# Four query and key tiles of a two-layer transformer step move into neighbourhood attention's first twelve steps

## Time and profile before

| | |
|---|---|
| median of 3 runs | 2887.59 us (2887.43 to 2888.29) |
| the profiled execution | its span 2885.2 us, 2.4 us below the median of the runs |
| PE, PEld busy | 2841.8 us (98%), 2658.3 us (92%) |
| DVE, ACT, POOL busy | 2112.8 us (73%), 1190.9 us (41%), 347.7 us (12%) |
| input projection from its fourth tile | 508.9 to 593.9 us |
| V projection | 593.9 to 622.4 us |
| neighbourhood attention, 20 steps | 622.4 to 672.5 us |
| its output projection | 672.5 to 700.8 us |

### The profile page before, as it was taken

The page is one execution under the profiler, slowest core; times in us unless marked ns, Lnnn a source line. Parts: engine busy times, 40 slices in busy tenths (PEclk is TensorE's granted clock), DMA queues, the critical chain, the costliest instruction groups (busy, mean ns, idle before and its releaser), DMA issues. The chain is left out here.

```text
span 2885.2 us, 46747 instructions
## 1 busy us (share of the span) xinstructions
PE 2841.8 (98%) x18154; PEld 2658.3 (92%) x18154; DVE 2112.8 (73%) x4053; ACT 1190.9 (41%) x2212; POOL 347.7 (12%) x436
## 2 busy tenths in 40 slices
PE   8999999999999999999999999999999999999998
PEld 5999999978789999999999998798887988999998
DVE  5898987766768989778878775755747467866856
ACT  5433535254666334356334354223233144533433
POOL 1000003120031000021000022202112033000001
PEclk9999999999999999999999999999999999999999
DMA  7544343521014433424433222324223231422221
GB/s 258 147 150 132 107 127 119 180 74 47 23 46 131 152 119 105 130 79 116 130 100 103 92 96 94 111 94 125 68 87 116 81 132 37 105 78 88 76 86 66
DMA packets 94238, 303.52 MB, mean 105 GB/s; under 512 B 10753, under 2 KB 21281, under 8 KB 93121
## 3 DMA queue, kind: packets, MB, share of 16 engines
q1 hardware_dynamic: 67328, 223.03, 23.8%
q0 software_dynamic: 21296, 63.58, 8.0%
q10 hardware_dynamic: 5392, 13.92, 1.3%
HBM read 285.14 MB, written 7.49 MB: 101 GB/s over the span
## 5 line engine op out<-in xcount | busy, mean ns | idle before, releaser
L2566 PE MATMUL ps<-g,w 128*128 128x320 f32 x4224 | 624.8, 308 | 0.0
L2566 PEld LDWEIGHTS ps<-g,w 128*128 128x128 f32 x4224 | 620.6, 187 | 0.8
L2533 PE MATMUL ps<-h,w 128*128 128x320 f32 x3744 | 578.3, 309 | 8.4 <-ACT swu L1022 4.6
L2533 PEld LDWEIGHTS ps<-h,w 128*128 128x128 f32 x3744 | 556.0, 188 | 10.3 <-ACT swu L1022 5.7
L2533 PE MATMUL ps<-e,w 128*128 128x320 f32 x2808 | 437.3, 309 | 0.1
L2533 PEld LDWEIGHTS ps<-e,w 128*128 128x128 f32 x2808 | 418.2, 188 | 0.4 <-DMA e<-tsum 0.4
L1541 DVE TENSOR_TENSOR w<-raw,w 128x1024 fp32r<-128x1024 f32 (+1 forms) x243 | 277.5, 1146 | 160.9 <-ACT w L915 144.7
L2714 PE MATMUL ps<-w,h 128*128 128x512 f32 x1596 | 367.4, 391 | 0.1
L2714 PEld LDWEIGHTS ps<-w,h 128*128 128x128 f32 x1596 | 298.1, 188 | 62.7 <-ACT rg L1486 1.0
L928 ACT ACTIVATE w<-w2s 128x512 fp32r<-128x512 f32 x312 | 194.1, 631 | 275.2 <-DVE w2s L1693 84.2
L915 ACT ACTIVATE w<-raw 128x1024 fp32r<-128x1024 f32 x123 | 128.9, 1061 | 264.2 <-PE ps L2400 130.9
(11 more groups left out here) (305 smaller groups left out, 3672.4 us busy)
## 6 DMA issues: line engine op xcount, KB each, us to landing
raw<-in_ws SPq DMA_DIRECT2D x303, 512.0 KB, 3.7
cond<-in_ada POOLq DMA_DIRECT2D x80, 512.0 KB, 3.9
raw<-in_ws SPq DMA_DIRECT2D x96, 384.0 KB, 3.1
raw<-in_ada SPq DMA_DIRECT2D x32, 512.0 KB, 3.6
cond_em<-in_ada POOLq DMA_DIRECT2D x16, 512.0 KB, 3.9
e<-tsum POOLq DMA_DIRECT2D x12, 640.0 KB, 6.3
ada<-in_ada SPq DMA_DIRECT2D x5, 1024.0 KB, 17.9
rst<-in_state ACTq DMA_DIRECT2D x4, 1024.0 KB, 4.8
```

The source lines that it names most:

```text
L2533: mm = pe.matmul(ps[:, 4 * s + bank, 0:HT], w2[:, at // 2, wi, c:c + P], rhs(k, ri), start=start and k + wi + ri == 0, stop=(k == 3 and wi ...
L2566: mm = pe.matmul(pair_half(pr, half), w2[:, slot_of(n), wi, c:c + P], half_of(g2[:, k, ri, :], half), start=k + wi + ri == 0, stop=(k == n ...
```

## The change

- The block order becomes: five latent tiles, query tiles 0 and 1, key tiles 0 and 1, the rotary tile, V, then query and key tiles 2 and 3 (heads 4 to 7). The projection has 10 tiles in place of 14; squares, sums and broadcasts move up by as many.
- The last four tiles are projected in token halves of 320, eight halves of eight groups of three matmuls, all in bank 7. The 64 groups are dealt over the first twelve steps: eight ahead of step 0's transposes, then two or three ahead of the transposes and two or three behind them. A half starts when the one before it is evacuated; ACT evacuates halves 0, 1, 4, 5, DVE halves 2, 3, 6, 7.
- The four blocks are split by ACT and DVE around the first units and at units 8 and 14, the output projection's first two among them. DVE's copies of V tile 4 go behind unit 2 in place of unit 3.
- The context output goes to 128 free columns of bank 5, and ACT copies it twice (`octx`), so that DVE reads its rest from there. V tile 4 goes to bank 6.
- The latents are split behind neighbourhood attention: ACT's high parts ahead of its splits for the output projection, DVE's low parts between its additions.
- Three condition blocks and two memsets move behind the rotary key on DVE, the last condition load behind the power on POOL. Two bias buffers and the conditions' row lie in 12 KB that a smaller descriptor area for POOL's transfers leaves free.

```diff
-EM_PAIR = [0, 1, 3, 2, 0] + [(e - 4) % 3 for e in range(5, 14)]
-V_BANK = [2, 3, 4, 5, 7]
+EM_PAIR = [0, 1, 3, 2, 0, 1, 2, 0, 1, 0]
+EM_SQUARES = {3: (0,), 4: (1,), 5: (2,), 6: (3,), 7: (4,)}
+EM_SUMS = {4: (0, 1), 5: (2,), 6: (3,), 7: (4,)}
+V_BANK = [2, 3, 4, 5, 6]
+DENSE_SLOTS = [(8, 0)] + [((3, 2), (3, 3), (2, 3))[i % 3] for i in range(10)] + [(3, 0)]
+DENSE_ACT = (0, 1, 4, 5)
+DENSE_SPLITS = {8: 18, 14: 19}
+LATENTS = (3, 4, 0, 1, 2)
...
 ACT, behind the first units
             exp_unit(1, True)
+            split(n0 + EM_V + 6)
...
+            dense_outs(0)
             pt_evac(0, True)
             pt_evac(1, True)
+            split(n0 + EM_V + 7)
             for g in range(2, NU):
                 exp_unit(g, True)
+                if g % 2 == 0 and g >= 4:
+                    dense_outs(g - 2)
                 if g >= 4:
                     pt_evac(g - 2, True)
...
+            for j in LATENTS:
+                latent_hi(j)
             for m in range(4):
                 split(n0 + 18 + m + LEAD, (n0 + 18 + m + LEAD) % RING)
...
 DVE
                 normalise(g)
-                if g == 3:
-                    dve.wait_ge(wt_free, done(n0 + 17))
+                if g == 2:
+                    dve.wait_ge(wt_free, done(n0 + EM_V + 3))
                     v_rows(5, slice(0, P), 4)
                     v_rows(3, high, 4, low).then_inc(v_odd, 1)
+                    split(n0 + EM_V + 6)
+                if g == 3:
+                    split(n0 + EM_V + 7)
...
+                dense_outs(g - 2)
+                if g - 1 in DENSE_SPLITS:
+                    split(n0 + DENSE_SPLITS[g - 1])
...
             for j in range(4):
                 split(n0 + 18 + j + LEAD)
+                if j:
+                    for c in ((), LATENTS[0:2], LATENTS[2:4], LATENTS[4:])[j]:
+                        latent_lo(c)
                 dve.wait_ge(wt_free, done(n0 + 18 + j))
...
 PE
+            def dense_step(i):
+                d, k = divmod(i, KD)
+                j, h = divmod(d, 2)
+                n = n0 + EM_DENSE + j
+                if k == 0:
+                    if h == 0:
+                        have(n)
+                    if d:
+                        pe.wait_ge(em_ev, EM_TILES - 1 + d)
+                for wi, ri in ((0, 0), (0, 1), (1, 0)):
+                    mm = pe.matmul(ps[:, 7, 0:HT], w2[:, slot_of(n), wi, k * P:(k + 1) * P],
+                                   half_of(h2[:, k, ri, :], h), start=(k == 0 and wi == 0 and ri == 0),
+                                   stop=(k == KD - 1 and wi == 1))
+                if k == KD - 1:
+                    mm.then_inc(wt_free if h else dense_mm, 1)
...
                 for g in range(0, NU, 2):
                     if g + 4 < NU:
                         pair_scores(g + 4)
+                    dense(g // 2, 0)
...
                     weight_mm(g, True)
                     weight_mm(g + 1, True)
+                    dense(g // 2, 1)
+                    if g % 10 not in (0, 2):
                         pair_values(g - 2, True)
...
+            pe.wait_ge(c_lo, 5)
             tok_tiles(n0 + 22, 1, lambda k, ri: ckv2[:, k, ri, :], 2, range(6), lambda t: 2 + t,
-    nc = bacc.Bacc("TRN2", target_bir_lowering=False, num_devices=1)
+    nc = bacc.Bacc("TRN2", target_bir_lowering=False, num_devices=1, dynamic_dma_scratch_size=4096)
```

More of the change, by code:

```diff
@@ L69 @@
 FFN_AT.append(NBLOCKS)
-EM_PAIR = [0, 1, 3, 2, 0] + [(e - 4) % 3 for e in range(5, 14)]
-V_BANK = [2, 3, 4, 5, 7]
+EM_PAIR = [0, 1, 3, 2, 0, 1, 2, 0, 1, 0]
+EM_TILES = len(EM_PAIR)
+EM_V = EM_TILES
+EM_DENSE = EM_V + 4
+EM_SQUARES = {3: (0,), 4: (1,), 5: (2,), 6: (3,), 7: (4,)}
+EM_SUMS = {4: (0, 1), 5: (2,), 6: (3,), 7: (4,)}
+V_BANK = [2, 3, 4, 5, 6]
+DENSE_SLOTS = [(8, 0)] + [((3, 2), (3, 3), (2, 3))[i % 3] for i in range(10)] + [(3, 0)]
+DENSE_END = [sum(map(sum, DENSE_SLOTS[:i])) + sum(DENSE_SLOTS[i][:v + 1]) for i in range(len(DENSE_SLOTS))
+             for v in range(2)]
+DENSE_HALVES = 8
+LATENTS = (3, 4, 0, 1, 2)
+DENSE_ACT = (0, 1, 4, 5)
+DENSE_SPLITS = {8: 18, 14: 19}
+DENSE_AT = {next(i for i, end in enumerate(DENSE_END) if end >= KD * (d + 1)): d for d in range(DENSE_HALVES)}
 NA_WINDOW = {1: (0, 192), 2: (64, 256), 3: (192, 256), 4: (320, 192)}
@@ L812, in _ @@
             norm_pow(1)
-            for b in range(2, ADA_EM):
+            for b in range(2, ADA_EM - 1):
                 condition_load(ADA_FFN[0] + b)
@@ L1190, in _ @@
             act.dma_start(ckvr[:, :, 0:PAST], a["cache_ckv"]).then_inc(em_ld2, 16)
-            for e in range(13):
+            for e in range(EM_TILES - 1):
                 if e > 1:
[L1193 to L1203, removed]
+                    split(n0 + e + LEAD)
+                for j in EM_SQUARES.get(e, ()):
                     act.wait_ge(em_ev, j + 1)
@@ L1208, in _ @@
                     act.activation(esq[:, j % 2, :], src, ACT.Square).then_inc(esq_done, 1)
-            act.wait_ge(em_ev, 13)
-            for e in range(4):
+                act.wait_ge(wt_free, done(n0 + e))
+                src = pair(EM_PAIR[e])
+                if 5 <= e < 7:
+                    act.activation(qa[e - 5], src, ACT.Copy, scale=NAD ** -0.5).then_inc(em_ev, 1)
+                else:
+                    dst = cqr[:, e, :] if e < 3 else ckvr[:, e - 3, PAST:] if e < 5 else ka[:, e - 7, PAST:]
+                    act.activation(dst, src, ACT.Copy).then_inc(em_ev, 1)
+            act.wait_ge(em_ev, EM_TILES - 1)
+            for e in range(2):
                 act.dma_start(a["new_k"][:, e], ctx_of(ka[:, e, PAST:])).then_inc(out_done, 16)
-            for j in range(3):
-                split(n0 + 13 + j + LEAD, (n0 + 13 + j + LEAD) % RING)
-            act.wait_ge(wt_free, done(n0 + 13))
+            for n in range(EM_TILES + 1, EM_TILES + 4):
+                split(n0 + n)
+            act.wait_ge(wt_free, done(n0 + EM_TILES - 1))
             act.dma_start(va_na[4], a["cache_v"]).then_inc(em_ld, 16)
@@ L1232, in latent_hi @@
                     act.activation(ckv2[:, j - 3, 0, :], ckvr[:, j - 3, :], ACT.Copy).then_inc(c_hi, 1)
[L1234 to L1243, removed]
+            split(n0 + EM_V + 4)
+            split(n0 + EM_V + 5)
             def exp_unit(g, na):
@@ L1324, in _ @@
             act.wait_ge(pv_mm, NU)
-            o_ctx(3)
+            na_ctx(3)
+            act.wait_ge(em_ev, EM_TILES - 1 + DENSE_HALVES)
+            for e in range(2, 4):
+                act.dma_start(a["new_k"][:, e], ctx_of(ka[:, e, PAST:])).then_inc(out_done, 16)
+            for j in LATENTS:
+                latent_hi(j)
             for m in range(4):
@@ L2072, in _ @@
             rstd_diag(NT, 1, e_var, e_pow, e_diag, NT)
-            split(n0 + 13 + LEAD)
-            dve.wait_ge(wt_free, done(n0 + 13))
+            split(n0 + EM_TILES + 1)
+            dve.wait_ge(wt_free, done(n0 + EM_TILES - 1))
             dve.wait_ge(e_rb, 2)
@@ L2683, in _ @@
             halves((n0, n0 + 1, n0 + 2), EM_PAIR[0:3], 1)
-            for e in range(3, 14):
+            for e in range(3, EM_TILES):
                 if e >= 4:
@@ L2810, in pair_values, with dense @@
                             mm.then_inc(pv_mm, 1)
+            def dense_step(i):
+                d, k = divmod(i, KD)
+                j, h = divmod(d, 2)
+                n = n0 + EM_DENSE + j
[10 more added lines that the diff above has]
+                    mm.then_inc(wt_free if h else dense_mm, 1)
+            def dense(i, v):
+                if i < len(DENSE_SLOTS):
+                    at = 2 * i + v
+                    for step in range(DENSE_END[at - 1] if at else 0, min(DENSE_END[at], KD * DENSE_HALVES)):
+                        dense_step(step)
             def attend_pairs():
@@ L3187, in stream_blocks @@
         put(tiles(wi[:, o + e * P:o + (e + 1) * P]))
-    for e in range(8):
+    for e in (0, 1, 4, 5):
         put(tiles(wi[:, e * P:(e + 1) * P]))
@@ L3192, in stream_blocks @@
     token_major(wi[:, 2 * na:3 * na])
+    for e in (2, 6, 3, 7):
+        put(tiles(wi[:, e * P:(e + 1) * P]))
     wo = w["mix_w_out"][0]
```

122 lines of the change are left out of this document (79 added, 43 removed).

## The result

The changed kernel takes 2892.30 us (median of 20 runs, 2889.63 to 2896.63) against 2887.55 for the kernel before on the same chips: 4.75 us more, ratio 1.0017 with a 95% interval of 1.0012 to 1.0023. The forecast was 2889.6, range 2882.9 to 2894.5, and "same within 0.2%" its likeliest case. The time is inside the range, at its upper part, and inside the 0.2%; the interval says that the kernel is slower and not equal.

What follows compares the result with a forecast made beforehand. TensorE, busy 98% of the span, bounds the kernel, so only its waits matter. Moved matmuls cancel (-28.0 + 28.0) and small terms sum to +2.0 us on 2885.2; with 2.4 us to the runs' median, 2889.6 us, range 2882.9 to 2894.5.

Steps and rivals of the forecast that it cites:

- Edits taken at nothing, (a): Norm's chain moved four tiles forward: diagonal ready at 556.2, PE at broadcast at 556.7, so hidden; 0 (0 to 1.5 us).
- Steps 0 and 1: First two attention steps: PE waits 0.9 us for unit 2, 3.2 for unit 3; wait grows 2.0 to 4.1, +2.1.
- The clock: Attention, after the new 3.2 us PE wait: loss from a fall to half clock, a third taken, +0.4 us (0 to 2).
- Waits for an evacuation: Step 5: half 4 waits until VectorE has evacuated half 3 from bank 7; +1.1 us (0 to 1.5).
- Gaps and changes of kind: PE's gaps in steps 2 to 11 go, -3.7 us; dense groups in 22 places add 0.1 each, +2.2 us.
- The last eight steps: End of neighbourhood attention: both engines start ahead, so part of 1.03 us of PE waits goes; -0.4 us (0 to -1).
- Behind attention: Output projection to latent projection: last latent low part ends about when PE asks for it; +0.3 us (0 to 2).
- (f), the descriptor area: POOL's software transfers: smaller area keeps every other address, at most three transfers are open at once; 0.
- (1): Rival: dense work fills everything, no wait in steps 0 and 1, changes of kind free; -4.7 us, 2882.9; chance 0.15.
- (2): Rival: dense groups empty the array in 22 places at 0.32 us, 7.0 instead of 2.2; 2894.4; chance 0.08.
- (3): Rival: each half waits for its evacuation as half 3 does, seven times 1.1 us; 2896.2; chance 0.04.
- (4): Rival: the change does not hide its work, every gap stays and groups only add; +6.1 us, 2893.7; chance 0.05.

Runs made afterwards that it cites:

- experiment 2: Changed kernel with VectorE's two copies of V tile 4 behind unit 3 and its split parts behind units 4 and 5: 2888.56 us, ratio to before 1.0006.
- experiment 3: Changed kernel with half 3 evacuated by ScalarE and ScalarE's split of block 19 at unit 13 instead of 14: 2891.91 us, ratio to before 1.0013.
- experiment 11: The changed kernel as it is, run once more: 2892.29 us, ratio to before 1.0015.
- experiment 1: Changed kernel with the latents' variance one condition block earlier and POOL's last two condition loads behind the power: 2891.29 us, ratio to before 1.0012.
- experiment 6: Kernel of experiment 4 with ten more places for dense groups, one group behind each step's first unit's transposes: one run, 2882.37 us.
- experiment 8: Kernel of experiment 4 with dense groups shifted in steps 0 and 11, more of them behind the transposes: 2884.88 us, ratio to before 0.9990.
- experiment 5: Kernel before the change with only the smaller descriptor area (4096) for POOL's transfers: 2887.24 us, ratio 1.0001.
- experiment 9: Kernel of experiment 8 with the first latent's ten sums behind tile 3, apart from the second's: 2882.59 us, ratio to before 0.9982.
- experiment 4: Changed kernel with the edits of experiments 1, 2 and 3, plus ScalarE's split of block 17 behind unit 4's exponential: 2884.78 us, ratio to before 0.9989.
- experiment 7: Kernel of experiment 4 with 184 of the 192 moved dense matmuls left out, evacuations and waits kept: attention takes 58.19 us.

## Why the forecast came out 2.7 us low, term by term

The case was the forecast's: the moved matmuls cancel and small terms decide. The sum was +2.0; in the profile it is +5.45 for these stretches, in the medians +4.75. Of what it said would show it, the wait in step 1 (3.04 us) and the one behind half 3 (0.97) came. A projection without a wait did not, and attention takes 81.75 us (595.58 to 677.33), where 79.1 to 80.1 were named. Its own signs of being wrong came true twice: the ten steps run at 4.85 us each (4.7 was the bound), and the clock stays low for some 3.4 us (3). That the range held is luck in part: in the profile four terms came out 4.3 us above the forecast together, and three others 0.9 below it.

- **Edits taken at nothing, (a): 0 became 1.86.** This is the largest miss, a term that was put at nothing; its bound of 1.5 was passed in the profile. I had counted "hidden by half a microsecond" from the one execution of before, in which VectorE waited at most 0.53 for a load. The four profiles with this chain (the first, experiments 2, 3 and 11) show that the landing of the loads varies and that the wait is 0 to 1.72 us; half a microsecond is no margin over a chain of 13 loads, each waiting for the block two before.
- **Steps 0 and 1: +2.1 became +2.0** (3.70 us of waits against 1.70). The forecast had 0.9 us for unit 2 and 3.2 for unit 3; it is 0.66 and 3.04, for the reason given: this was the forecast's best mechanism, and experiment 2 confirms it.
- **The clock: +0.4 became +1.5.** It fell behind the 3.04 us. I weighed the dense groups close ahead of the wait as holding it; they did not. In the other profiles with that wait (experiments 1, 3 and 11) it fell as well. The Trainium skill's page "TensorE: Matmul & The Clock Gate", section "Part 1: The HAM clock gate", has the slow clock as the default that activity lifts, which the forecast read as a sure fall. The traces agree at 3.04 us of wait (four of four), and at waits of 0.65 and 0.49 (experiment 2) they show 1.00 throughout.
- **Waits for an evacuation: +1.1 became +1.73.** Half 3's was 0.97. Half 5's (0.76) I had missed: I had counted what PE does between two halves, and not that ScalarE's split of block 19 stands ahead of half 4's evacuation (experiment 3).
- **Gaps and changes of kind: -3.7 + 2.2 became -2.0.** This is what is left of the twelve steps when the other terms are taken off. The net was near, both terms too large. A change of kind costs 0.03 where it was measured (experiment 6) and not 0.1: a gap counted from start to start holds the end of the transposes, which nothing can fill but which a dense group behind them does not pay again. The idle time of the busy view, 2.32 us for these steps, was the nearer count. The same Trainium skill page, section "Step-by-step: what each phase is for", gives 0 for a change of kind by its rule that weights load ahead; the trace has 0.03, nearer to that than the row that I took.
- **The last eight steps: -0.4 became +0.34.** No engine starts ahead: VectorE's scores wait for the transposes four units back, which stand behind the dense groups. Experiment 8 shows it: two groups shifted take 0.84 us off.
- **Behind attention: +0.3 became 0.** The last low part ended at 704.3, PE asked at 705.59.
- **(f), the descriptor area**, costs nothing in the kernel before (experiment 5). Of the rivals, (1) is what the kernel of experiment 9 reaches (2882.59, forecast 2882.9) once the orders are mended, though by other terms: -1.5 in steps 0 and 1, -1.9 in steps 2 to 11, -0.5 in the last eight, against -2.0, -3.7 + 1.1 and -0.4; (2) is out by experiments 4 and 6; (3) happened for two halves; (4) is out, since experiment 4 has no waits where before had 2.32 us.

## What to carry to other kernels

Work moved into an engine's gaps was worth about those gaps as its idle time shows them, a few microseconds here, and each queue that it brings work to can take them back: list, for each engine, what stands ahead of the instruction that the bound engine waits for next. A chain that had time to spare before the move has to be given its margin again; one trace shows one landing of its loads and not the spread. A single wait of 3.04 us on TensorE was paid here one and a half times or more, once as a wait and once in the clock.

## What the runs showed of the hardware

- After the 3.04 us wait the granted clock fell from 1.00 to 0.50 (2.4 to 1.2 GHz) in four profiles of four, in three during the wait, in one 0.9 us behind it. It stayed there for 3.4 to 6.8 us, most of it under full PE work. From the transposes behind the wait to the values PE took 4.65 to 5.83 us, against 3.26 at a clock of 1.00 (experiment 2): 1.4 to 2.6 us lost.
- In experiment 7, where PE was busy for 6.84 of 10.62 us, the clock also fell behind a wait of 1.84 us, and again behind one of 2.08.
- A run of matmuls of one column can take the clock down although PE shows no wait: 1.5 us lost at the end of twenty, in three of nine profiles, and of forty in the one that there is; with ten it was not seen in three.
- VectorE's wait for one and the same of the like condition loads was 0.47 to 0.53 us in six profiles and 0.95 to 2.03 in six others.
